# Splitting the merged tiles one by one, sending the last projection's tiles singly, and storing the result in eight transfers

## The reference, cut to what matters

```python
y_a = (o_a * jax.nn.silu(dsa_z)) @ w_up_a[layer]
...
y_b = (o_b * jax.nn.silu(gdn_z)) @ w_up_b[layer]
merged = jax.nn.sigmoid(gate_a) * y_a + jax.nn.sigmoid(gate_b) * y_b
x = x + merged @ w_out[layer]
...
return _rmsnorm(x, final_norm_w)
```

## Time and profile before

| what | us |
|---|---|
| median of three runs | 2921.03 |
| lowest and highest of them | 2919.41, 2924.48 |
| the profiled execution | 2915.46 |
| its span, first to last instruction | 2913.7 |
| mean granted clock of TensorE, share of full | 0.966 |

### The profile page before, as it was taken

One profiled execution on the slowest core, in us unless ns is written; L12 is line 12 of the kernel. 1 busy time (PEld: TensorE's weight loads), 2 busy tenths in 40 slices (PEclk: granted clock), 3 DMA queues, 4 the chain that ended last, 5 costly groups with the idle time before them and its releaser, 6 DMA issues.

```text
span 2913.7 us, 42233 instructions
## 1 busy us (share of the span) xinstructions
PE 2755.8 (95%) x17756; PEld 2246.5 (77%) x17756; DVE 1490.7 (51%) x1826; ACT 966.6 (33%) x1464; POOL 200.5 (7%) x271
## 2 busy tenths in 40 slices
PE   6999999898999999999999889999999999968996
PEld 5888877687888878888777778888777777558775
DVE  6565666745565443333457543333355557655533
ACT  3222234523222232222345223222324445232322
POOL 3000000410000000000002300000000000022000
PEclk9999999989999999999999889999999999879998
DMA  7565542103565222232221012232321221100231
GB/s 285 196 228 202 187 152 76 44 17 110 200 211 214 83 98 101 79 115 79 88 87 62 3 58 101 84 109 81 109 94 58 80 73 66 47 2 3 76 108 44
DMA packets 45513, 299.68 MB, mean 103 GB/s; under 512 B 5552, under 2 KB 5680, under 8 KB 16944
## 3 DMA queue, kind: packets, MB, share of 16 engines
q1 hardware_dynamic: 36144, 230.35, 22.8%
q0 software_dynamic: 9216, 67.11, 6.3%
HBM read 295.35 MB, written 2.10 MB: 102 GB/s over the span
## 4 chain that ended last, share of the span: by engine, by line
PE 89%; DVE 7%; ACT 2%; DMA 1%; issue 1%; POOL 0%; SPq 0%; DVEq 0%; ACTq 0%; POOLq 0%
PE ps L917 17%; PE ps L918 17%; PE ps L919 17%; PE ps L1205 6%; PE ps L1206 5%; PE ps L1207 5%; PE ps L1512 2%; PE ps L1513 2%; PE ps L1514 2%; PE ps L2041 1%; PE ps L2025 1%; PE ps L2038 1%; DMA ada_first<-in_ada 1%; DVE w_lo L894 1%; PE ps L1327 1%
## 5 line engine op out<-in xcount | busy, mean ns | idle before, releaser
L917 PE MATMUL ps<-hn_hi,w_hi 128*128 128x512 f32 x1536 | 603.1, 393 | 36.1 <-DVE hn_lo L867 17.0
L918 PE MATMUL ps<-hn_lo,w_hi 128*128 128x512 f32 x1536 | 601.7, 392 | 0.0
L919 PE MATMUL ps<-hn_hi,w_lo 128*128 128x512 f32 x1536 | 601.2, 391 | 0.0
L894 DVE TENSOR_TENSOR w_lo<-w_raw,w_hi 128x2048 fp32r<-128x2048 f32 (+3 forms) x229 | 472.4, 2063 | 180.6 <-ACT w_hi L887 177.1
L887 ACT ACTIVATE w_hi<-w_raw 128x2048 fp32r<-128x2048 f32 (+3 forms) x229 | 394.5, 1723 | 115.8 <-PE ps L1207 97.4
L917 PEld LDWEIGHTS ps<-hn_hi,w_hi 128*128 128x128 f32 x1536 | 291.1, 190 | 100.1 <-issue 39.4
L919 PEld LDWEIGHTS ps<-hn_hi,w_lo 128*128 128x128 f32 x1536 | 290.8, 189 | 61.1
L918 PEld LDWEIGHTS ps<-hn_lo,w_hi 128*128 128x128 f32 x1536 | 291.1, 189 | 60.2
L1205 PE MATMUL ps<-hn_hi,w_hi 128*128 128x512 f32 x776 | 323.6, 417 | 7.7 <-DVE hn_lo L867 4.9
L1206 PE MATMUL ps<-hn_lo,w_hi 128*128 128x512 f32 x776 | 306.5, 395 | 0.0
L1207 PE MATMUL ps<-hn_hi,w_lo 128*128 128x512 f32 x776 | 306.0, 394 | 0.0
(11 more groups left out here) (449 smaller groups left out, 3384.9 us busy)
## 6 DMA issues: line engine op xcount, KB each, us to landing
w_raw<-in_up SPq DMA_DIRECT2D x88, 1024.0 KB, 4.8
ada_w<-in_ada POOLq DMA_DIRECT2D x64, 1024.0 KB, 5.1
w_raw<-in_down SPq DMA_DIRECT2D x64, 704.0 KB, 4.0
w_raw<-in_mix_in SPq DMA_DIRECT2D x20, 1024.0 KB, 4.8
w_raw<-in_dsa_in SPq DMA_DIRECT2D x18, 1024.0 KB, 4.8
w_raw<-in_merge SPq DMA_DIRECT2D x16, 768.0 KB, 4.2
ada_first<-in_ada SPq DMA_DIRECT2D x8, 1024.0 KB, 12.6
w_raw<-in_mix_out SPq DMA_DIRECT2D x8, 1024.0 KB, 4.8
```

The lines of the kernel that those rows point to most:

```text
L894: dve.tensor_tensor(w_lo[:, slot, 0:size], w_raw[:, slot, 0:size], w_hi[:, slot, 0:size].bitcast(F32), ALU.subtract).then_inc(w_lo_ready, 1)
L917: pe.matmul(bank, wh, x_hi[:, k], start=(k == 0), stop=False)
L918: pe.matmul(bank, wh, x_lo[:, k], start=False, stop=False)
L919: return pe.matmul(bank, wl, x_hi[:, k], start=False, stop=(k == K - 1))
```

## The change

Four things, all behind the recurrence:

1. The tiles of `mg` are rounded one at a time, in part 1 of the merge: ACT writes tile i-1 into `mg_hi` and DVE tile i-1 into `mg_lo` in the course of piece i, and tile 7 behind the last. These are tiles of their own, so nothing that PE still reads is overwritten. The loops over the pieces of part 1 on ACT and DVE become straight code.
2. The first piece of the last projection goes by k (both t for each k, `by_k`) and waits for tile k of `merged` rather than for one signal.
3. In the last piece t = 0 signals `first_done` on its own; ACT, DVE and the square of tile 6 follow it while PE makes t = 1. The sums over `rstd` and over tile 6's square stand among PE's products of t = 1, after k = 5. DVE adds tile 7 straight from its bank once `piece_done` rises.
4. Each of the eight final multiplications raises `h_final`, and SP issues a transfer for each tile.

```diff
+        mg_hi = tiles("mg_hi", 0, 8, dt=F32R)
+        mg_lo = tiles("mg_lo", 38, 8, dt=F32R)
...
-            sp.wait_ge(h_final, 1)
-            sp.dma_start(out, mg[:]).then_inc(stored, 16)
-            sp.wait_ge(stored, 16)
+            for j in range(KD):
+                sp.wait_ge(h_final, j + 1)
+                sp.dma_start(out[:, j], mg[:, j]).then_inc(stored, 16)
+            sp.wait_ge(stored, 16 * KD)
...
-            for i in range(4):
-                pe_piece(pe, p0 + i, (p0 + i) % 2, KD, 2, hn_hi, hn_lo, lambda k: None if i or k else pe.wait_ge(merged, 1))
-            norm_sums(pe, nn)
+            for i in range(3):
+                pe_piece(pe, p0 + i, (p0 + i) % 2, KD, 2, mg_hi, mg_lo, lambda k: None if i else pe.wait_ge(merged, k + 1), by_k=i == 0)
+            p, slot = p0 + 3, (p0 + 3) % 2
...
+            for t in range(2):
+                for k in range(KD):
...
+                    if t and k == KD - 3:
+                        pe.wait_ge(sq_added, SQ_ADDS * nn)
+                        token_sums(pe, rstd[:], True, False)
+                        norm_sum(pe, nn, KD - 2)
+                last.then_inc(piece_done if t else first_done, 1)
+            norm_sum(pe, nn, KD - 1)
+            norm_spread_pe(pe, nn)
...
+                    if part and i:
+                        act.wait_ge(dve_evac, p0 + i)
+                        act.activation(mg_hi[:, i - 1], mg[:, i - 1], ACT.Copy).then_inc(merged_hi, 1)
                     act.wait_ge(piece_done, p0 + i + 1)
...
-                if part:
-                    steps(act, KD, piece)
-                else:
-                    for i in range(KD):
-                        piece(i, i % 2)
+                for i in range(KD):
+                    piece(i, i % 2)
             act.wait_ge(dve_evac, start_of["merge", 1] + KD)
-            act.activation(hn_hi[:], mg[:], ACT.Copy).then_inc(merged_hi, 1)
+            act.activation(mg_hi[:, KD - 1], mg[:, KD - 1], ACT.Copy).then_inc(merged_hi, 1)
...
-                act.wait_ge(piece_done, p0 + i + 1)
+                if i < 3:
+                    act.wait_ge(piece_done, p0 + i + 1)
+                else:
+                    act.wait_ge(first_done, len(narrow_pieces) + 1)
...
-            act.wait_ge(dve_evac, p0 + 4)
-            norm_square(act, 3 * LAYERS + 1, KD - 2)
-            norm_square(act, 3 * LAYERS + 1, KD - 1)
+            for t in range(2):
+                act.wait_ge(dve_evac, p0 + 4 + t)
+                norm_square(act, 3 * LAYERS + 1, KD - 2 + t)
...
-            dve.wait_ge(merged_hi, 1)
-            dve.tensor_tensor(hn_lo[:], mg[:], hn_hi[:].bitcast(F32), ALU.subtract).then_inc(merged, 1)
+                        if i:
+                            merged_low(i - 1)
+
+                def merged_low(j):
+                    dve.wait_ge(merged_hi, j + 1)
+                    dve.tensor_tensor(mg_lo[:, j], mg[:, j], mg_hi[:, j].bitcast(F32), ALU.subtract).then_inc(merged, 1)
...
+            merged_low(KD - 1)
...
                     hj = h[:, 2 * i + t]
+                    if t and i == 3:
+                        last.then_inc(dve_evac, 1)
+                        dve.wait_ge(piece_done, p0 + 4)
                     last = dve.tensor_tensor(hj, hj, tmp[:, s] if t == 0 else main[s][1], ALU.add)
...
-                last = dve.scalar_tensor_tensor(mg[:, j], h[:, j], v2("final", j), small[0], ALU.mult, ALU.mult)
-            last.then_inc(h_final, 1)
+                dve.scalar_tensor_tensor(mg[:, j], h[:, j], v2("final", j), small[0], ALU.mult, ALU.mult).then_inc(h_final, 1)
```

More of the change, by code:

```diff
@@ L1531, in second_pe @@
             nn = 3 * LAYERS + 1
-            for i in range(4):
-                pe_piece(pe, p0 + i, (p0 + i) % 2, KD, 2, hn_hi, hn_lo, lambda k: None if i or k else pe.wait_ge(merged, 1))
-            norm_sums(pe, nn)
+            for i in range(3):
+                pe_piece(pe, p0 + i, (p0 + i) % 2, KD, 2, mg_hi, mg_lo, lambda k: None if i else pe.wait_ge(merged, k + 1), by_k=i == 0)
+            p, slot = p0 + 3, (p0 + 3) % 2
+            pe.wait_ge(w_lo_ready, p + 1)
+            pe.wait_ge(act_evac, p - 1)
+            pe.wait_ge(dve_evac, p - 1)
+            for t in range(2):
+                for k in range(KD):
+                    col = (2 * k + t) * P
+                    wh, wl = w_hi[:, slot, col:col + P], w_lo[:, slot, col:col + P]
+                    bank = main[slot][t]
+                    pe.matmul(bank, wh, mg_hi[:, k], start=(k == 0), stop=False)
+                    pe.matmul(bank, wh, mg_lo[:, k], start=False, stop=False)
+                    last = pe.matmul(bank, wl, mg_hi[:, k], start=False, stop=(k == KD - 1))
+                    if t and k == KD - 3:
[5 more added lines that the diff above has]
+            norm_spread_pe(pe, nn)
         def second_act(act):
```

## The result

| what | before | after |
|---|---|---|
| median of four executions, us | 2921.91 | 2895.19 |
| lowest to highest of them | 2919.41 to 2924.48 | 2893.79 to 2897.58 |
| profiled execution | 2915.46 | 2895.92 |
| its span | 2913.7 | 2894.2 |
| span counted from ACT's last sigmoid of the merge | 75.4 | 57.9 |

The ratio is 0.9916, 95% interval 0.9894 to 0.9938: the changed kernel is faster, and by more than was forecast. The direction was right; the range was not.

The account below looks back on a forecast made before the run. PE bounds the kernel (89% of the chain), so gains lie only in its idle or slow-clock time and the end: 11.9 + 1.0 + 3.5 = 16.4 us off the median 2921.0 gives 2904.6 us, range 2898.5 to 2911.

Parts of the forecast that it names:

- the handover: Merge to last projection: PE goes straight on, first piece done at 2849.16 instead of 2861.07; gain 11.9 us.
- The tail: Behind the last product: tile 7 alone remains, 3.0 us gained less 2.0 for sums among products; net gain 1.0 us.
- Sums among products: Last piece on PE: eight instructions, sixteen in the trace, moved into PE's stream add 2.0 us (bounds 1.9 and 3.6).
- no stall at tile 6's square: Last piece: tile 6's square ready at 7.5 us, PE wants it at 10.5; no stall, 3 us of slack.
- last product to root: Tail, last product to ACT's root: 3.27 us instead of 6.29, with 1.79 for the eight sums.
- The store: Program's end: eight stores under the multiplications, last landing 2.8 us instead of 6.3; gain 3.5 us (1.2 to 4.0).
- The crowded store: Rival, final stores: last tile's transfer lands in 5.1 us behind its elders, total 2906.9 us; chance 0.12.
- The growth: Sign of being wrong, final stores: issue-to-landing time grows from the first store to the eighth; no size given.
- The sum: Behind the recurrence: 11.9 + 1.0 + 3.5 = 16.4 us gained in all.
- the fast rival: Rival, tail: tile 7's sums take 1.05 instead of 1.79 us, last transfer saves 0.5; 2903.4 us, chance 0.12.
- serial stores: Rival, SP's queue: each store begins after the previous landed; 2919.5 us (even, chance 0.03) or 2937.9 (slower, chance 0.03).
- late handover: Rival, last projection's start: PE still waits for tile 7, 3.5 us idle plus up to 1.3 slow; 2909.4 us, chance 0.06.

## Why the prediction was right and wrong

**What bounds the kernel, the handover (right).** The working said that PE would go straight on, its first piece ending 10.88 us behind the merge; it did, to 0.01 us. Tile 7's remainder came at 2839.75, 3.4 us behind the sigmoid's start, as worked out, and 4.5 us before PE needed even tile 6. Gain forecast 11.9, in the trace 11.9. What the working did not see is that the 1.6 of slow start in the 11.9 is a matter of chance: 1.6 to 1.7 us in three profiles with the gap, 3.0 and 3.1 in two.

**The tail (right, small).** Sums among products forecast at 2.0 us, measured 1.8; no stall at tile 6's square; last product to root forecast 3.27, measured 2.92, because the eight sums took 1.44 and not 1.79. Net 1.0 forecast, 1.6 in the two traces, 0.5 in the kernel with the tail undone. The value taken lies between; the rows gave no way to do better.

**The store (term mis-sized).** The last landing was put at 2.8 us by a line through 512 KB and 2048 KB; it is 2.2 (2.07 for the first of the eight), which is below even the lower bound of 2.3. The line went through a load and a store; the two stores alone, 2.2 us for 256 KB and 6.3 for 2048, would put 512 KB at 2.8 us, where the load took 3.3. Why a load takes longer is not shown. The gain is 4.0, not 3.5. The crowded store did not occur: eight landings of 2.1 to 2.2 us, issued 0.66 us apart, so that they overlap three deep. The growth that the prediction named as a sign of being wrong is there, but it is under 0.2 us from the first to the eighth. The estimate in the prediction from the Trainium skill, page "DMA: Bandwidth & Descriptors", was 2.6 us and likewise high, by 0.4 us; by its section title the page's measurements are of loads issued from GpSimd, and these are stores issued from SP. The rule of the same page, section "Measured (HBM→SBUF, 128 partitions, SWDGE, issued from GpSimd)", to batch to 1 MiB or more was no guide here, where the data come in at 0.66 us a tile: what counted was the size of the last transfer alone.

**The sum**: 16.4 forecast, 17.5 in the traces, 17.2 by the ratio of 0.9941. This part of the prediction stands.

**The step that failed** is the one from the sum to a median and its range: "so I take it off the median", with a range "widened by the scatter of medians", which was read off three executions. Three times between 2919.4 and 2924.5 looked like a kernel that scatters by 5 us, and the profiled 2915.5 like a curiosity. The lower end, 2898.5, lies 4.9 us below the fast rival's 2903.4; taking off the whole 5.6 us of the profiled execution would have given 2897.8, still above the 2895.2 measured. The 73 executions run from 2910.5 to 2935.6. Of the 9.4 us between forecast and result, 1.1 are the sum (17.5 instead of 16.4); 2.7 are a base of 2921.0 where 73 executions give 2918.3; and 5.6 are the four executions of the changed kernel, whose median of 2895.2 lies below 2918.3 - 17.5 = 2900.8, while eight later ones gave 2899.35. This split takes the 73 later executions for what the kernel before does in the long run; the four beside the result had a median of 2921.9. That the four executions of the changed kernel were fast ones is supported by their clock, 0.967 to 0.969, and is otherwise put down to chance. The first comparison's ratio of 0.9916 overstated the gain; 17.5 us would be 0.9940, just above its interval's upper end of 0.9938, and 0.9941 was measured next.

That the scatter goes with the clock is shown by the fourteen profiles and by the correlation over 73 executions; where it arises, by two pairs of profiles. Why the clock stands at half for longer in one execution than in the next stays open; no edit here was aimed at it.

**The rivals.** The faster tail occurred in part (sums of 1.44 us, between 1.05 and 1.79, and a last store 0.6 lower than taken). No serial stores, no late handover. None of the rivals was about the base, and one should have been.

## What to carry to other kernels

When a kernel's executions scatter by more than the change is worth, measure the change as a stretch between two instructions that bracket it, and do not take the scatter from three or four executions: the range of a forecast has to cover both medians, not only the terms of the sum. A whole-tensor step between two stages that both go by tiles cost its own length here and a slow start of PE behind it; make it by tiles in the cover of the first stage, and let the second wait tile by tile. At the program's end only the last store's own landing counted here, so it pays to store in the units in which the data come; no size other than one tile and all eight was tried.

## What the runs showed of the hardware

- The mean granted clock of one and the same program ran from 0.956 to 0.967 in 73 executions, with times from 2935.6 to 2910.5 us. In the profiles compared the differences arise where PE works in bursts and in the first microseconds of the run of products behind them: over 2700 to 2740 us, with PE busy all 40 us, one profile had 0.91 and another 1.00. From 1800 to 2100 us it was 1.00 in the three profiles looked at.
- Behind an idle of 1.4 us on PE the next eight sums took 1.44, 1.42, 1.31 and 1.25 us in four profiles and 1.05 us in two. With products of no use in the wait they took 1.05 us in both kernels that had them.
- Behind an idle of 10.3 us PE's products ran at half clock at first in all five profiles, at a cost of 1.6 to 3.1 us; with 36 products of no use in that gap and 2.1 us of idle left, they did not.
- Eight stores of 256 KB, issued 0.66 us apart on one queue, each landed 2.1 to 2.2 us behind its issue; one of 2048 KB took 6.3.
